# A two-phase form of the 31-tap filter in `conv_taps`, with its gate and weight split on VectorE and the modulation units placed between column groups

## The reference, cut to what matters

```python
a, g = jnp.split(h @ pw1_w + pw1_b, 2, axis=-1)
u = a * jax.nn.sigmoid(g)
u = lax.conv_general_dilated(u, dw_w[:, None, :], window_strides=(1,),
                             padding=[(CONV_PAD, CONV_PAD)], ..., feature_group_count=d) + dw_b
u = jax.nn.silu(layernorm(u, ln_g, ln_b))
return u @ pw2_w + pw2_b
```

## Time and profile before

| | |
|---|---|
| median of 3 runs | 3328.24 us (3327.05 to 3329.19) |
| profiled execution, its own time | 3323.5 us |
| its span | 3321.9 us |
| busy in the span: PE, VectorE, ACT, POOL | 2565.6, 2097.9, 1406.0, 512.9 us |
| `conv_taps`, from VectorE's first memset to its last sum | 118.44 to 588.45 us |

### The profile page before, as it was taken

The page is one execution under the profiler, slowest core; times in us unless marked ns, Lnnn a source line. Parts: engine busy times, 40 slices in busy tenths (PEclk is TensorE's granted clock), DMA queues, the critical chain, the costliest instruction groups (busy, mean ns, idle before and its releaser), DMA issues. The chain is left out here.

```text
span 3321.9 us, 40914 instructions
## 1 busy us (share of the span) xinstructions
PE 2565.6 (77%) x13098; PEld 2050.7 (62%) x13098; DVE 2097.9 (63%) x1722; ACT 1406.0 (42%) x1455; POOL 512.9 (15%) x499
## 2 busy tenths in 40 slices
PE   4587770595399999999933998978494499999980
PEld 1466660484278888888832886757473388888860
DVE  2399999455476767588526001338554588888865
ACT  0211110443166666577523112434322277777752
POOL 0133320100000010001033000045200101001004
PEclk7688885796599999999965999989796699999995
DMA  8244330224188889799654211013454499999965
GB/s 301 92 153 153 126 107 20 96 76 172 42 322 311 322 320 327 280 349 385 264 219 172 100 48 52 20 53 109 172 194 147 153 376 382 393 383 391 394 254 215
DMA packets 297755, 701.18 MB, mean 211 GB/s; under 512 B 22640, under 2 KB 50096, under 8 KB 297654
## 3 DMA queue, kind: packets, MB, share of 16 engines
q1 hardware_dynamic: 259082, 570.79, 47.5%
q0 software_dynamic: 22656, 75.60, 6.4%
q10 hardware_dynamic: 15936, 53.75, 4.3%
HBM read 610.05 MB, written 91.06 MB: 211 GB/s over the span
## 5 line engine op out<-in xcount | busy, mean ns | idle before, releaser
L1394 DVE TENSOR_TENSOR moe_w_lo<-moe_w_raw,moe_w_hi 128x2048 fp32r<-128x2048 f32 x384 | 862.0, 2286 | 83.8 <-ACT moe_w_hi L1323 48.7
L1323 ACT ACTIVATE moe_w_hi<-moe_w_raw 128x2048 fp32r<-128x2048 f32 x384 | 714.8, 1909 | 63.9 <-issue 37.6
L653 DVE SCALAR_TENSOR_TENSOR taps_acc<-taps_u,taps_vec,taps_acc 128x1295 f32<-128x1295 f32 x232 | 387.2, 1744 | 0.0
L98 PE MATMUL moe_pg<-moe_w_hi,moe_xt_hi 128*128 128x512 f32 x592 | 243.8, 412 | 11.2 <-DVE moe_xt_lo L1405 5.9
L98 PE MATMUL moe_py<-moe_w_hi,moe_at_hi 128*128 128x512 f32 x592 | 241.6, 408 | 11.9 <-DVE moe_w_lo L1394 8.2
L99 PE MATMUL moe_pg<-moe_w_lo,moe_xt_hi 128*128 128x512 f32 x592 | 237.0, 400 | 0.0
L100 PE MATMUL moe_pg<-moe_w_hi,moe_xt_lo 128*128 128x512 f32 x592 | 236.8, 400 | 0.0
L99 PE MATMUL moe_py<-moe_w_lo,moe_at_hi 128*128 128x512 f32 x592 | 235.2, 397 | 0.0
L100 PE MATMUL moe_py<-moe_w_hi,moe_at_lo 128*128 128x512 f32 x592 | 234.8, 397 | 0.0
L100 PE MATMUL moe_pu<-moe_w_hi,moe_xt_lo 128*128 128x512 f32 x592 | 234.3, 396 | 0.0
L98 PE MATMUL moe_pu<-moe_w_hi,moe_xt_hi 128*128 128x512 f32 x592 | 234.1, 396 | 0.0
(11 more groups left out here) (305 smaller groups left out, 5366.0 us busy)
## 6 DMA issues: line engine op xcount, KB each, us to landing
moe_w_raw<-in_moe_w SPq DMA_DIRECT2D x384, 1024.0 KB, 12.6
taps_ada_w<-in_ada_w SPq DMA_DIRECT2D x40, 1024.0 KB, 7.0
scratch_experts_out<-moe_y ACTq DMA_DIRECT2D x57, 512.0 KB, 6.4
norm_x<-scratch_residual SPq DMA_DIRECT2D x28, 512.0 KB, 3.3
scan_v<-scratch_gla_values SPq DMA_DIRECT2D x20, 512.0 KB, 4.0
scratch_experts_in<-norm_h POOLq DMA_DIRECT2D x18, 512.0 KB, 3.0
comb_x<-scratch_residual SPq DMA_DIRECT2D x18, 512.0 KB, 6.9
ada_w<-in_ada_w SPq DMA_DIRECT2D x4, 2048.0 KB, 28.0
```

What stands on the lines that cost most here:

```text
L98: pe.matmul(out, xh, wh, start=start, stop=False)
L653: dve.scalar_tensor_tensor(acc[q][:, :], u[b][:, k:k + CONV_OUT], vec[b][:, k:k + 1], acc[q][:, :], ALU.mult, ALU.add).then_inc(s(f"tap{q} ...
L1323: act.activation(hi[m][:, cut, :], raw[m][p][:, cut, :], ACT.Copy).then_inc(s(f"{m}_hi{h}"), 1)
L1394: dve.tensor_tensor(lo[m][:, cut, :], raw[m][p][:, cut, :], hi[m][:, cut, :].bitcast(F32), ALU.subtract).then_inc(s(f"{m}_lo{h}"), 1)
```

## The change

**Two phases.** The input `u` is kept as two rows of even and odd samples, E and O. With tap weights w, an even output is the sum over j of (w[2j] + w[2j+1])·O[m+j] and of w[2j]·(E − O)[m+j]. An odd output is the same first sum, and the sum of w[2j+1]·(E[m+j+1] − O[m+j]). So the first sum is computed once (`shared`, 16 instructions, weights in `both`), then 16 instructions of `even` and 15 of `odd`, each over 649 elements where there were 1295, with the differences in `back` and `ahead`. `join` adds the two running sums twice per channel, into every second column of `vt`.

**Engines.** `gate` is one VectorE instruction per group: it reads `za` from PSUM, adds the bias, multiplies by `sg` and writes to the two rows of `u`. `low` moves to VectorE too. ACT's copy of `za` is gone, and POOL only issues the stores.

**Units.** The bias enters `ada_acc` as a product of a row of ones with `ada_b`, 4 matmuls more per unit, and ACT copies the sum into one of five `ada_row` buffers. From the second channel on, units stand behind single groups; in the first, all three still follow group 2. The loops are written out.

```diff
+EVEN, ODD = (TAPS + 1) // 2, TAPS // 2
+HALF_OUT = CONV_OUT // 2
...
-        ada_b = ph.sb("ada_b", [P, P])
-        ada_sum = ph.sb("ada_sum", [P, P])
-        ada_row = ph.sb("ada_row", [P, P])
...
+        ada_b = ph.sb("ada_b", [1, N])
+        one = ph.sb("one", [1, 2])
+        ada_row = [ph.sb(f"ada_row{j}", [P, P]) for j in range(len(ADA_UNITS))]
...
+        u = [ph.sb(f"u{b}", [P, 2, CONV_W // 2]) for b in range(2)]
+        back = ph.sb("back", [P, CONV_W // 2])
+        ahead = ph.sb("ahead", [P, CONV_W // 2 - 1])
+        acc = [ph.sb(f"acc{q}", [P, HALF_OUT]) for q in range(2)]
...
+        def units_behind(n, g):
+
+            units = units_of(n)
+            if n == 0:
+                return units if g == 2 else []
+            return units[g:g + 1] if len(units) == 3 else units[g - 1:g] if g else []
...
-                def low(b, i):
-                    pool.wait_ge(s(f"w_hi{b}"), i + 1)
-                    pool.tensor_tensor(w.lo[:, :, :, :], raw[b][:, :, :, :], w.hi[:, :, :, :].bitcast(F32),
-                                       ALU.subtract).then_inc(s(f"w_lo{b}"), 1)
-
-                def gate(b, i):
-
-                    for g, (t0, n, c0) in enumerate(CONV_GROUPS):
-                        pool.wait_ge(s(f"sig_ready{g}{b}"), i + 1)
-                        pool.wait_ge(s(f"a_ready{g}{b}"), i + 1)
-                        pool.tensor_tensor(u[b][:, c0:c0 + n], u[b][:, c0:c0 + n], sg[g][:, 0:n], ALU.mult)\
-                            .then_inc(s(f"u_ready{g}{b}"), 1)
...
-                        pool.tensor_tensor(ada_row[:, :], ada_sum[:, :], ada_b[:, :], ALU.add)\
-                            .then_inc(s("ada_out"), 1)
...
+                    for j4 in range(N // P):
+                        pe.matmul(ada_acc[j4 * STRIP:j4 * STRIP + 2, 0:P], one[:, :], ada_b[:, j4 * P:(j4 + 1) * P],
+                                  start=True, stop=False)
...
+                for n in range(KC):
+                    pe.wait_ge(s("w_lo"), n + 1)
+                    for g, (t0, m, _) in enumerate(CONV_GROUPS):
+                        if n:
+                            pe.wait_ge(s(f"sig_ready{g}"), n)
+                            pe.wait_ge(s(f"u_ready{g}"), n)
...
+                        last.then_inc(s(f"z_ready{g}"), 1)
+                        for at in units_behind(n, g):
+                            unit(at)
...
+                high(0)
+                act.wait_ge(s("vecs_ready"), 1)
+                for n in range(KC):
+                    for g, (t0, m, c0) in enumerate(CONV_GROUPS):
+                        act.wait_ge(s(f"z_ready{g}"), n + 1)
+                        if n:
+                            act.wait_ge(s(f"u_ready{g}"), n)
+                        act.activation(sg[g][:, 0:m], zg[g][:, 0:m], ACT.Sigmoid, bias=vecs[:, n, V_BG:V_BG + 1])\
+                            .then_inc(s(f"sig_ready{g}"), 1)
+                        if g == 2 and n + 1 < KC:
+                            high(n + 1)
+                        for at in units_behind(n, g):
+                            take(at)
 
...
+                dve.tensor_tensor(both[:, :, 0:ODD], vecs[:, :, 0:2 * ODD:2], vecs[:, :, 1:2 * ODD:2], ALU.add)\
+                    .then_inc(s("both_ready"), 1)
+                dve.tensor_copy(both[:, :, ODD:EVEN], vecs[:, :, TAPS - 1:TAPS]).then_inc(s("both_ready"), 1)
+
+                def low(n):
+                    dve.wait_ge(s("w_hi"), n + 1)
+                    dve.tensor_tensor(w.lo[:, :, :, :], raw[n % 2][:, :, :, :], w.hi[:, :, :, :].bitcast(F32),
+                                      ALU.subtract).then_inc(s("w_lo"), 1)
+
+                def gate(n):
+
+                    for g, (t0, m, c0) in enumerate(CONV_GROUPS):
+                        dve.wait_ge(s(f"z_ready{g}"), n + 1)
+                        dve.wait_ge(s(f"sig_ready{g}"), n + 1)
+                        dve.scalar_tensor_tensor(
+                            u[n % 2][:, :, c0 // 2:(c0 + m) // 2].rearrange("p q m -> p m q"),
+                            za[g][:, 0:m].rearrange("p (m q) -> p m q", q=2), vecs[:, n, V_BA:V_BA + 1],
+                            sg[g][:, 0:m].rearrange("p (m q) -> p m q", q=2), ALU.add, ALU.mult)\
+                            .then_inc(s(f"u_ready{g}"), 1)
+
+                def shared(n, j):
...
+                    src, tap = u[n % 2][:, 1, j:j + HALF_OUT], both[:, n, j:j + 1]
+                    if j == 0:
+                        dve.tensor_scalar(acc[0][:, :], src, tap, None, ALU.mult).then_inc(s("sum0"), 1)
+                    else:
+                        dve.wait_ge(s("sum0"), n * (EVEN + EVEN // 2) + j)
+                        dve.scalar_tensor_tensor(acc[0][:, :], src, tap, acc[0][:, :], ALU.mult, ALU.add)\
+                            .then_inc(s("sum0"), 1)
...
+                def even(n, j):
+
+                    src, tap = back[:, j:j + HALF_OUT], vecs[:, n, 2 * j:2 * j + 1]
...
+                def odd(n, j):
+
+                    src, tap = ahead[:, j:j + HALF_OUT], vecs[:, n, 2 * j + 1:2 * j + 2]
...
+                    dve.tensor_tensor(vt[:, n, parity:CONV_OUT:2], acc[0][:, :], acc[1][:, :], ALU.add)\
+                        .then_inc(s(name), 1)
...
+                low(0)
+                dve.wait_ge(s("u_zero"), 2)
+                dve.wait_ge(s("both_ready"), 2)
+                gate(0)
+                for n in range(KC):
...
-                    dve.tensor_scalar(acc[0][:, :], u[b][:, 0:CONV_OUT], vec[b][:, 0:1], vec[b][:, V_DWB:V_DWB + 1],
-                                      ALU.mult, ALU.add).then_inc(s(f"tap0{b}"), 1)
-                    dve.tensor_scalar(acc[1][:, :], u[b][:, 1:1 + CONV_OUT], vec[b][:, 1:2], None, ALU.mult)\
-                        .then_inc(s(f"tap1{b}"), 1)
-                    for k in range(2, TAPS):
-                        q = k % 2
-                        dve.wait_ge(s(f"tap{q}{b}"), i * len(range(q, TAPS, 2)) + k // 2)
-                        dve.scalar_tensor_tensor(acc[q][:, :], u[b][:, k:k + CONV_OUT], vec[b][:, k:k + 1],
-                                                 acc[q][:, :], ALU.mult, ALU.add).then_inc(s(f"tap{q}{b}"), 1)
-                    for q in range(2):
-                        dve.wait_ge(s(f"tap{q}{b}"), n * len(range(q, TAPS, 2)))
-                    dve.tensor_tensor(vt[:, ds(i * 2 + b, 1), :].rearrange("p o n -> p (o n)"), acc[0][:, :],
-                                      acc[1][:, :], ALU.add).then_inc(s("taps_summed"), 1)
...
+                        dve.wait_ge(s(f"u_ready{g}"), n + 1)
+                    if n:
+                        dve.wait_ge(s("odd_done"), n)
+                    dve.tensor_tensor(back[:, :], u[n % 2][:, 0, :], u[n % 2][:, 1, :], ALU.subtract)\
+                        .then_inc(s("back"), 1)
+                    shared(n, 0)
+                    if n == 0:
+                        low(1)
+                    dve.tensor_tensor(ahead[:, :], u[n % 2][:, 0, 1:], u[n % 2][:, 1, 0:CONV_W // 2 - 1], ALU.subtract)\
+                        .then_inc(s("ahead"), 1)
+                    even(n, 0)
+                    for j in range(1, EVEN):
+                        shared(n, j)
+                        even(n, j)
+                    join(n, 0, "even_done", 0)
+                    if n + 1 < KC:
+                        gate(n + 1)
+                    dve.wait_ge(s("even_done"), n + 1)
+                    for j in range(ODD):
+                        odd(n, j)
+                        if j == 3 and n + 2 < KC:
+                            low(n + 2)
+                    join(n, 1, "odd_done", 1)
```

More of the change, by code:

```diff
@@ L506, in _ @@
[L506 to L519 removed]
+                    pool.memset(u[b][:, :, :], 0.0).then_inc(s("u_zero"), 1)
@@ L521, in _ @@
+                for j in range(per_pair):
+                    pool.wait_ge(s(f"stored{j}"), 32 * (total // per_pair))
             @block.tensor
@@ L669, in conv_taps @@
+                dve.wait_ge(s("odd_done"), KC)
         ph.close()
```

258 lines of the change are left out of this document (94 added, 164 removed).

## The result

The changed kernel takes **3278.55 us** (median of 4 runs, 3274.61 to 3279.33) against 3328.72 for the kernel before in the same measurement: a ratio of 0.985, interval 0.9837 to 0.9862, 50.2 us less. The profiled executions, 3279.33 and 3323.5, differ by 44.2.

The account below looks back on a forecast made before the run. VectorE's own time was taken as the bound. Filter from 165.9, channel 0 to 229.6, five channels of 44.1, then 41.9 and 40.2: end 532.2 against 588.45, 56.2 us gained; profiled 3267.3, median 3272 us, range 3262 to 3292.

Parts of the forecast that it names:

- The tap's step, 0.805 us of 649 elements: VectorE's filter taps follow each other at 0.805 us; 44 of them make 35.4 us a channel.
- The weighing of the fixed cost: VectorE instructions: 0.13 us fixed in a step by the trace, against the skill's 58 cycles, which would give 3248 us.
- The tensor_scalar, 0.47 a step: Three tensor_scalar instructions of VectorE's filter in each channel, 0.47 us a step, together 1.4 us.
- the waits at the joins and at `back`: VectorE waiting for its own last result at the two joins and `back`: 0.3 us a channel.
- The gate, 1.7 us a channel: Gate on VectorE: 0.40 us for group 0, 0.66 for each of groups 1 and 2, strided stores at full pace.
- half pace: Rival: strided stores of gates and joins run at half pace, costing 20 us, 3292 us; 10 in 100.
- The rule on 16-byte lines: Skill's rule for SBUF access: crossing to a new 16-byte line pays a penalty, so the gate would cost more per element.
- POOL's hold, 6.9 us of 53.3: VectorE and POOL wait for each other over SBUF in the taps: 6.9 us of a 53.3 us channel.
- The stall of 17.4 us at channel 1: VectorE waits 17.4 us at channel 1's gate, inside channel 0, because PE does three units first.
- The rival of a late PE, and its slack of 4.0 us: PE, with 4.0 us slack in three-unit channels, becomes late through clock drops at units: 15 us, 3287; 8 in 100.
- The clock's rival: PE's clock stays low through both 512-groups behind units: 79 us lost, 3351 us, slower than before; 3 in 100.
- The sum against the median: Forecast of the profiled execution, 3267.3 us, plus 4.7 because the median of the runs stood that much above: 3272 us.

Follow-up runs that it names:

- e_gate_order: Changed kernel with each gate walking all even elements first, then all odd ones, so that it writes two contiguous runs: 3273.22 us.
- e_gate_pe_order: Changed kernel with TensorE reading its moving operand at every second element, so that the gate reads and writes contiguous runs: 3448.68 us.
- e_engines_only: Changed kernel with the single-phase filter of before; gate and split stay on VectorE: 3321.00 us.
- e_phase_only: Changed kernel with gate and weight split back on POOL; the two-phase filter stays: 3286.08 us.
- e_no_units_first: Changed kernel without units in channel 0: three behind the groups of channels 1 to 6, two in channel 7; 3269.63 us.
- e_plan: Changed kernel with units replanned per channel, channel 1's gate and channel 2's split behind odd tap 5 of channel 0, gates written in runs: 3256.83 us.
- e_units_last: Changed kernel with the units of every channel behind its last group, none between groups: 3274.18 us.

## Why the prediction was right, and what was off

It was 3272, with 3262 to 3292 as the range; 3278.6 came. That the median is only 6.6 us off is in part luck: the profiled execution was forecast at 3267.3 and came at 3279.3, 12.0 more, of which 7.6 are in the stage, 2.0 in its later start and 2.4 behind it, where the work is the same. Taken from the stage's start, its end was forecast at 413.8 us (532.2 − 118.4) and came at 421.4: 7.6 us late, of which 1.7 are in channel 0 and 5.9 in the seven others.

- *The tap's step, 0.805 us of 649 elements.* Right: instructions of 0.89 that follow each other at 0.805 (238.25, 239.05, 239.85 in the changed kernel). This is the largest term, 35.4 us a channel, and with it the gain stands or falls. The weighing of the fixed cost fell to the trace's side: by 58 cycles it would have been 0.736.
- *The tensor_scalar, 0.47 a step.* Slightly mis-sized: one steps by 0.47 and two by 0.52 (0.556 to 0.617 us long instead of 0.55), 0.1 us a channel. With the waits at the joins and at `back`, 0.55 us instead of 0.3, a channel is about 0.3 us longer, 2 us in all.
- *The gate, 1.7 us a channel.* This is the term that failed in size: 0.49 + 0.92 + 0.92 (260.93, 261.42, 262.34, and the next row at 263.26) are 2.3 us, 0.6 more. That is 3.7 us in channels 1 to 6, the larger part of the 5.9; the gate of channel 1, in channel 0, adds another 0.6 and gate(0), which everything waits for, some 0.5. I had set the store that jumps between two rows at full pace and named half pace as the rival. It is neither: 0.34 us more for 512 elements, 45% over the 0.742 of e_gate_order, and e_gate_order shows that it is the store's pattern. The join, which writes every second element of one row, runs at full pace (0.836, forecast 0.84).
- *The rule on 16-byte lines.* The Trainium skill (SBUF — State Buffer, "Door 1: The DMA port swizzle") wants two hits in each line for full pace, and that section gives no price for leaving it. The gate's store leaves its line at each element and pays; the join's store and e_gate_order's reads of SBUF, at every second fp32, have two hits and run at full pace: so far the runs agree. The moving operand of e_gate_pe_order has two hits in a line as well and runs at half pace (0.45 against 0.227): there they don't, and the measurement decides.
- *POOL's hold, 6.9 us of 53.3.* Right in size: with gate and split on VectorE and the old taps a channel is 50.3 long (e_engines_only), which is 46.3 + 2.0 + 2.3 with 0.3 to spare, and the hold is gone. It would have stayed with the short taps: e_phase_only loses 7.2 us behind the joins of the channel shown, and POOL's gate is kept waiting for 16.83 us.
- *The stall of 17.4 us at channel 1.* 17.15, in the two pieces forecast, with chunk 1 starting at 184.52 (182.5 and the stage's 2.0 later start). e_no_units_first and e_plan show that it is PE's chain of units and chunk, and that it was to be had back.
- *The rival of a late PE, and its slack of 4.0 us.* It didn't come. The sigmoid of group 2 of channel 2 is done at 259.38 and wanted at 262.34: 3.0. A unit between groups took 2.25 us, not 2.1.
- *The clock's rival.* It didn't happen: the units between groups don't lower the clock. The windows of the start of channel 6 and of the rest of it, with its two units between groups, show the granted clock third from the right:

```profile
403.80:407.20 3.40, 3.40 (x18) 3.40 (x19) 3.40 (x5) 0.00 (x0) 0.00 (x0) 0.56 0.00 0
410.60:438.50 27.90, 27.90 (x276) 22.13 (x278) 27.73 (x36) 2.55 (x6) 2.25 (x4) 1.00 0.45 152
```

In the stage behind channel 0's groups the clock is low only where PE has waited, for the split (57.4 us in 7 waits) and, in channel 0, for the units' loads, and for a few us behind each wait. It is 1.00 through groups and units alike.

- *The sum against the median.* I added 4.7 us because the profiled execution of before lay that much under its median. After, it lies 0.8 above it. Of the 44.2 us between the profiled ones, the 48.6 of the stage are the change's; the later start and what lies behind the stage take 4.4 back. The 50.2 between medians hold differences of that kind too.

## What to carry to other kernels

Where an engine is full for a whole stage, count its instructions' elements first: half the length for 47 tap instructions in place of 31 was 43 of 49 us, and the engines' exchange, though it removed a hold of 7 us a channel, was 5, because the work that VectorE took over cost 4 a channel there (gate 1.7, split 2.2) and the first channel stalled. When work is placed into an order by hand, place the first rounds by themselves: the steady loop's order cost 17 us at the start. Moving three units out of the first channel brought 9 us there, while moving those of the later channels between or behind their groups left 45.0 us a channel (e_units_last). And work whose data has a single buffer should not stand twice in a row on the engine that the others wait for, however short its instructions are: each further unit cost 8 us instead of 2.3.

## What the runs showed of the hardware that I had not expected

- A VectorE store that alternates between two rows 2.7 KB apart: 1.08 us for 512 fp32 elements (0.65 for 256) against 0.742 (0.477) for two runs; reading at every second element, from PSUM and SBUF, 0.742. ScalarE's copy of 512 pays for the same store as well, 1.17 against 0.68.
- TensorE with a moving fp32 operand at every second element: 0.45 us for 512 columns against 0.227 at a granted clock of 1.00; at 0.50, 0.233 for 256 columns against 0.213.
- VectorE's taps of 649 elements, following each other at 0.805 us, kept a GpSimd subtraction of 448 elements that came while they ran out for 20.83 us and lost nothing themselves; the price came at the join, 1.6 us a channel for five of them. Where the subtraction came first, taps and subtractions took turns, and the taps took 1.56 us instead of 0.89. Taps of 1295 elements had let GpSimd in and lost 4.2 us to one split.
